# Seven block products for ten input-projection pairs per layer, with the weight sums on GpSimd

## The reference, cut to what matters

```python
h = modulate(rms_norm_2(x, norm1_g), shift1, scale1)
p = h @ w_in                                  # 1024 x 5376
p_ret  = p[..., :RET_COLS]                    # q, k, v, g of the retention mixer
p_rwkv = p[..., RET_COLS:RET_COLS + RWKV_COLS]
p_conv = p[..., RET_COLS + RWKV_COLS:]
q, k, v, g = jnp.split(p_ret, 4, axis=-1)     # rotary on q and k, then retention
gates = jax.nn.sigmoid((h @ w_gate + b_gate).astype(F32))
```

## Time and profile before

| | |
|---|---|
| median of 3 runs | 2393.79 us |
| profiled execution: time, span | 2393.09 us, 2391.3 us |
| TensorE busy | 2263.7 us (95%) |
| weight loads | 1509.1 us (63%) |
| VectorE, ScalarE, GpSimd busy | 675.4, 400.0, 391.6 us |
| granted TensorE clock, mean | 0.992 |

### The profile page before, as it was taken

The page is one execution under the profiler, slowest core; times in us unless marked ns, Lnnn a source line. Parts: engine busy times, 40 slices in busy tenths (PEclk is TensorE's granted clock), DMA queues, the critical chain, the costliest instruction groups (busy, mean ns, idle before and its releaser), DMA issues.

```text
span 2391.3 us, 29443 instructions
## 1 busy us (share of the span) xinstructions
PE 2263.7 (95%) x12878; PEld 1509.1 (63%) x12878; DVE 675.4 (28%) x1225; ACT 400.0 (17%) x787; POOL 391.6 (16%) x347
## 2 busy tenths in 40 slices
PE   9999999999999999999988888899999999888887
PEld 8776676676668888888333333378888863333333
DVE  5532224423216633423100000044443221000001
ACT  3320112620113320211000000033112020000001
POOL 2387631258752000000000000000000000000000
PEclk9999999999999999999999999999999999999999
DMA  7377731358752342349999999953333799999998
GB/s 276 111 310 285 302 137 72 128 213 342 300 202 80 109 141 89 106 160 403 422 428 428 427 428 427 415 197 127 106 108 106 278 406 427 428 428 428 427 428 317
DMA packets 136843, 654.65 MB, mean 274 GB/s; under 512 B 9864, under 2 KB 15112, under 8 KB 108168
## 3 DMA queue, kind: packets, MB, share of 16 engines
q1 hardware_dynamic: 136712, 652.72, 68.4%
HBM read 651.64 MB, written 1.05 MB: 273 GB/s over the span
## 4 chain that ended last, share of the span: by engine, by line
PE 76%; DMA 18%; DVE 2%; ACT 2%; SPq 1%; issue 1%; POOL 0%; DVEq 0%; ACTq 0%; POOLq 0%
PE bank L744 75%; DMA ring<-in_w_exp_up 11%; DMA PRGT<-in_w_exp_up 5%; DMA PRGT<-in_w_exp_down 1%; ACT R L3217 1%; SPq L658 1%; PE bank L1339 0%; DVE sm L2085 0%; POOL PRGT L3315 0%; ACT SQ L3257 0%; DVE PRGT L2416 0%; PE bank L930 0%; DVE PRGT L2079 0%; PE bank L1088 0%; DVE PRGT L2082 0%
## 5 line engine op out<-in xcount | busy, mean ns | idle before, releaser
L744 PE MATMUL bank<-hT,ring 128*128 128x256 f32 x3296 | 733.8, 380 | 0.0
L744 PEld LDWEIGHTS bank<-hT,ring 128*128 128x128 f32 x3296 | 619.8, 190 | 100.2 <-issue 15.3
L744 PE MATMUL bank<-PRGT,R 128*32 128x512 f32 x1120 | 275.9, 609 | 29.9 <-DMA PRGT<-in_w_exp_up 18.5
L744 PE MATMUL bank<-ring,R 128*32 128x512 f32 (+1 forms) x992 | 250.5, 587 | 39.9 <-DMA ring<-in_w_exp_up 25.0
L3393 POOL TENSOR_TENSOR SQ<-xT 128x512 f32<-128x512 f32 x4 | 4.2, 1056 | 1468.5 <-DVE xT L2808 1468.2
L744 PE MATMUL bank<-PRGT,SQ 128*32 128x512 f32 (+2 forms) x864 | 192.5, 530 | 15.6 <-ACT SQ L3257 12.2
L744 PE MATMUL bank<-PRGT,ring 128*128 128x256 f32 (+5 forms) x1136 | 197.0, 373 | 0.4 <-ACT PRGT L3014 0.4
L744 PEld LDWEIGHTS bank<-PRGT,R 128*32 128x32 f32 x1120 | 74.1, 112 | 194.4 <-issue 193.9
L744 PEld LDWEIGHTS bank<-PRGT,ring 128*128 128x128 f32 (+3 forms) x1136 | 163.2, 172 | 31.4 <-issue 3.0
L744 PEld LDWEIGHTS bank<-ring,R 128*32 128x32 f32 (+1 forms) x992 | 69.4, 114 | 168.1 <-issue 167.8
L744 PE MATMUL bank<-ring,SQ 128*32 128x512 f32 (+2 forms) x640 | 167.2, 519 | 8.3 <-ACT SQ L3257 8.3
(11 more groups left out here) (400 smaller groups left out, 2154.3 us busy)
## 6 DMA issues: line engine op xcount, KB each, us to landing
PRGT<-in_w_exp_gate SPq DMA_DIRECT2D x42, 2048.0 KB, 31.9
ring<-in_w_exp_up SPq DMA_DIRECT2D x36, 2048.0 KB, 31.9
ring<-in_mlp_w SPq DMA_DIRECT2D x32, 2048.0 KB, 8.8
PRGT<-in_w_exp_down SPq DMA_DIRECT2D x30, 2048.0 KB, 31.2
PRGT<-in_w_exp_up SPq DMA_DIRECT2D x28, 2048.0 KB, 31.8
PRGT<-in_w_ada SPq DMA_DIRECT2D x32, 1536.0 KB, 11.7
ring<-in_w_exp_down SPq DMA_DIRECT2D x24, 2048.0 KB, 33.3
ring<-in_w_exp_gate SPq DMA_DIRECT2D x22, 2048.0 KB, 32.1
```

The source lines that it names most:

```text
L744: return mm(o, lhsT=lhsT, rhs=rhs, start=first, stop=last, **kw)
```

## The change

Pairs 11 to 20 of each layer (SEVEN) are computed as a 2x2 block product. The contraction (1024 = 2 x 512) and the output (two tiles, and two token halves) are cut in two, and seven products of 512 x 128 x 128 replace eight, at the price of sums: four sums of the activations once a layer (`input_sums`), and four sums of weights a pair (`column_sums`), all on GpSimd and each followed by a semaphore wait of its own. Each product is 4 matmuls of 128 tokens. A pair takes two `acc` banks: four products go to the four 128-column regions of bank n, three go one after the other through the first 128 columns of bank n + 1 (`x`), each copied out by ScalarE (`corners_out`) to a corner buffer in SBUF before the next may overwrite or end it. The first half of a pair now holds four products and the second three. Within the first half the first two products need no sum of the weights, the third waits for the first sum, the fourth for the second.

VectorE puts the pair together (`joined`, three additions, each with one input in PSUM): `joined(10 + j // 2)` at the even steps from 2 on, before the rotary work of that step, then 18 before the turned XX is awaited, and 19 and 20 after the first two levels. GpSimd starts the weight sums behind the first ROWS of the stage; each pair's sums also wait for the weights and for the pair two before it to be nearly done; those of pair 15 also wait for `ret_kq`, the end of the rotary work. ScalarE's order of evictions moves a little. SP's condition for a next load becomes the last product of the pair. Two semaphores are folded into others to make room.

```diff
+SEVEN = tuple(range(11, 21))
...
+        k4 = lambda ap: ap.rearrange("p (k n) -> p k n", k=4)
+        HSUM = [k4(flat(GT[:, 10:12, :])), k4(flat(GT[:, 22:24, :])), k4(hsum3[:, :]), k4(flat(POOL_CD[:, 78:80, :]))]
+        WS = [[k4(flat(YB[:, 6 * b + 2 * r:6 * b + 2 * r + 2, :])) for r in range(3)] for b in range(2)]
+        CORNERS = [small_w[:, 640:1024], flat(stat[:, :, :])[:, 0:384]]
...
+        def h_block(kb, t):
+            return hT[:, 4 * kb:4 * kb + 4, t * P:(t + 1) * P]
+        def w_block(p, kb, h):
+            W = ring[2 + p // 2 % 2][:, 0:(SLOT if p < 20 else 2048)].rearrange("p (k n) -> p k n", k=KT)
+            c = (2 * (p % 2) + h) * P
+            return W[:, 4 * kb:4 * kb + 4, c:c + P]
+        def regions(o):
+            return (o[:, j * P:(j + 1) * P] for j in range(4))
...
+                def seven_products(p, h, o, n):
+                    g = seven_at(l, p)
+                    s1, s2, s4 = WS[g % 2]
+                    t1, t2, t3, t4 = HSUM
+                    z, y1, w, y = regions(o)
+                    m = n + 1
+                    x = acc[m % BANKS][:, 0:P]
+                    def product(dst, lhs, rhs, first=False):
+                        for k in range(4):
+                            ins = mul(dst, lhs[:, k, :], rhs[:, k, :], first and k == 0, False, skip_group_check=True)
+                        return ins
+                    if h == 0:
+                        if m >= BANKS:
+                            pe.wait_ge(dense_read[m % BANKS], m // BANKS)
+                        product(x, w_block(p, 0, 0), h_block(0, 0), True).then_inc(sems["corner_full"], 1)
+                        product(z, w_block(p, 1, 0), h_block(1, 0), True)
+                        pe.wait_ge(sems["sums_ready"], sums_at(l, p) + 1)
+                        product(y, s1, t1)
+                        pe.wait_ge(sems["sums_ready"], sums_at(l, p) + 2)
+                        pe.wait_ge(sems["corner_read"], 2 * g + 1)
+                        product(x, s2, t2).then_inc(sems["corner_full"], 1)
+                    else:
+                        product(w, w_block(p, 1, 1), t4)
+                        pe.wait_ge(sems["sums_ready"], sums_at(l, p) + 3)
+                        product(y1, s4, h_block(1, 1)).then_inc(dense_full[n % BANKS], 1)
+                        pe.wait_ge(sems["sums_ready"], sums_at(l, p) + 4)
+                        pe.wait_ge(sems["corner_read"], 2 * g + 2)
+                        product(x, w_block(p, 0, 1), t3).then_inc(dense_full[m % BANKS], 1)
...
+                def joined(p):
+                    b, full = pair_after(l, p)
+                    m, copied = sum_after(l, p)
+                    o, c = acc[b], CORNERS[seven_at(l, p) % 2]
+                    f0, f1 = (PR[:, in_tiles(p), :][:, h, :] for h in range(2))
+                    dve.wait_ge(dense_full[b], full)
+                    dve.wait_ge(dense_read[m], copied)
+                    v.tensor_tensor(f0, c[:, 0:2 * P], o[:, 0:2 * P], ALU.add)
+                    step(v.tensor_tensor(two(f1), bcast(c[:, 2 * P:3 * P], 2), two(o[:, 2 * P:4 * P]), ALU.add))
+                    v.tensor_tensor(f0[:, P:2 * P], f0[:, P:2 * P], o[:, 3 * P:4 * P], ALU.add).then_inc(dense_read[b], 1)
...
+                    if j >= 2 and j % 2 == 0 and 10 + j // 2 in SEVEN:
+                        joined(10 + j // 2)
...
+                joined(18)
...
+                    if lev < 2:
+                        joined(19 + lev)
...
+                def corners_out(p):
+                    g = seven_at(l, p)
+                    if p in SEVEN[2:]:
+                        b, full = pair_after(l, SEVEN[SEVEN.index(p) - 2])
+                        act.wait_ge(dense_read[b], full)
+                    m, full = sum_after(l, p)
+                    x, c = acc[m][:, 0:P], CORNERS[g % 2]
+                    act.wait_ge(sems["corner_full"], 2 * g + 1)
+                    f(c[:, 0:P], x, ACT.Copy).then_inc(sems["corner_read"], 1)
+                    act.wait_ge(sems["corner_full"], 2 * g + 2)
+                    f(c[:, P:2 * P], x, ACT.Copy).then_inc(sems["corner_read"], 1)
+                    act.wait_ge(dense_full[m], full)
+                    f(c[:, 2 * P:3 * P], x, ACT.Copy).then_inc(dense_read[m], 1)
...
-                for p in range(9, 15):
+                for p in range(9, 16):
                     evict(p)
-                    if p < 12:
-                        swap(p - 8)
+                    if p in (9, 10, 12):
+                        swap({9: 1, 10: 2, 12: 3}[p])
                 n0 = BANK_AT[f"ret_v{l}"]
                 for c in range(TT):
                     copy_out(n0 + c, VT[:, c * 512:(c + 1) * 512])
-                evict(15)
+                evict(16)
                 for p in (14, 15):
                     evicted(p)
                 act.wait_ge(sems["ret_kq"], L.nxt("ret_kq"))
                 f(flat(SIG), flat(PR[:, 12:16, :]), ACT.Sigmoid).then_inc(sems["g_sig"], 1)
-                evict(16)
                 n0 = BANK_AT[f"bonus{l}"]
                 for m in (n0, n0 + 1):
                     act.wait_ge(bank_full[m % BANKS], filled(m))
                 evict(17)
+                evict(18)
                 n0 = BANK_AT[f"turn{l}"]
                 for c in range(TT):
                     copy_out(n0 + c, XTH[c])
-                for p in range(18, 21):
+                for p in range(19, 21):
...
+            def input_sums(l):
+                pool.wait_ge(sems["norm_out"], 46 + KT * l)
+                n = BANK_AT[f"lora{l}"] + 3
+                pool.wait_ge(bank_full[n % BANKS], filled(n))
+                t1, t2, t3, t4 = HSUM
+                b11, b12, b21, b22 = h_block(0, 0), h_block(0, 1), h_block(1, 0), h_block(1, 1)
+                g.tensor_tensor(t1, b12, b11, ALU.subtract).then_inc(sems["sums_ready"], 1)
+                pool.wait_ge(sems["sums_ready"], sums_at(l) + 1)
+                g.tensor_tensor(t2, b22, t1, ALU.subtract).then_inc(sems["sums_ready"], 1)
+                pool.wait_ge(sems["sums_ready"], sums_at(l) + 2)
+                g.tensor_tensor(t3, b22, b12, ALU.subtract).then_inc(sems["sums_ready"], 1)
+                pool.wait_ge(sems["sums_ready"], sums_at(l) + 3)
+                g.tensor_tensor(t4, b21, t2, ALU.subtract).then_inc(sems["sums_ready"], 1)
+                pool.wait_ge(sems["sums_ready"], sums_at(l) + 4)
+            def column_sums(l, p):
+                n, q = seven_at(l, p), p // 2
+                u = SLOT_AT[(f"mid_even{l}", f"mid_odd{l}")[q % 2]][0][1] + q // 2
+                if p % 2 == 0 or p == SEVEN[0]:
+                    pool.wait_ge(slot_full[2 + q % 2], loaded(u))
+                if n >= 2:
+                    b, full = pair_after(*((l, SEVEN[SEVEN.index(p) - 2]) if p in SEVEN[2:] else (l - 1, SEVEN[SEVEN.index(p) - 2])))
+                    pool.wait_ge(dense_full[b], full)
+                s1, s2, s4 = WS[n % 2]
+                a11, a12, a21, a22 = w_block(p, 0, 0), w_block(p, 1, 0), w_block(p, 0, 1), w_block(p, 1, 1)
+                g.tensor_tensor(s1, a21, a22, ALU.add).then_inc(sems["sums_ready"], 1)
+                pool.wait_ge(sems["sums_ready"], sums_at(l, p) + 1)
+                g.tensor_tensor(s2, s1, a11, ALU.subtract).then_inc(sems["sums_ready"], 1)
+                pool.wait_ge(sems["sums_ready"], sums_at(l, p) + 2)
+                g.tensor_tensor(s4, a12, s2, ALU.subtract).then_inc(sems["sums_ready"], 1)
+                pool.wait_ge(sems["sums_ready"], sums_at(l, p) + 3)
+                g.tensor_tensor(a21, a11, a21, ALU.subtract).then_inc(sems["sums_ready"], 1)
+                pool.wait_ge(sems["sums_ready"], sums_at(l, p) + 4)
...
+                input_sums(l)
                 pool.wait_ge(sems["rw_ops"], l + 1)
                 nc.gpsimd.memset(S1[0:64, 256:512], 0.0)
                 nc.gpsimd.memset(S1[64:128, 0:256], 0.0).then_inc(sems["cleared"], 1)
+                pool.wait_ge(sems["cleared"], l + 4)
+                pool.wait_ge(sems["row_ready"], 15 * l + 1)
+                for p in SEVEN:
+                    if p == 15:
+                        pool.wait_ge(sems["ret_kq"], l + 1)
+                    column_sums(l, p)
```

More of the change, by code:

```diff
@@ L236, in nxt, with seven_at, sums_at @@
         return self.seen[name]
+def seven_at(l, p):
+    return len(SEVEN) * l + SEVEN.index(p)
+def sums_at(l, p=None):
+    return 4 * (len(SEVEN) + 1) * l + (0 if p is None else 4 * (SEVEN.index(p) + 1))
+USE_AT, _n = {}, 0
+for _l in range(DEPTH):
+    for _p in range((2, 1)[_l], PAIRS):
+        USE_AT[_l, _p] = _n
+        _n += 1 + (_p in SEVEN)
 def filled(n, i=0):
@@ L256, in pair_after, with sum_after @@
 def pair_after(l, p):
-    n = (PAIRS - 1) * l + p - 2
+    n = USE_AT[l, p]
+    return n % BANKS, n // BANKS + 1
+def sum_after(l, p):
+    n = USE_AT[l, p] + 1
     return n % BANKS, n // BANKS + 1
@@ L294, in build @@
         sm = sb("sm", [P, 512])
+        hsum3 = sb("hsum3", [P, 512])
         CW, W2, W3, ASG = 256, 320, 384, 448
```

(19 more changed lines are left out.)

6 lines of the change are left out of this document (3 added, 3 removed).

## The result

| | kernel before | changed kernel |
|---|---|---|
| median | 2394.0 us (8 runs) | 2401.67 us (8 runs, 2400.49 to 2404.12) |
| profiled execution: time, span | 2393.09, 2391.3 | 2400.49, 2398.7 |
| ratio of the times | | 1.0034, 95% interval 1.0024 to 1.0043 |

It is 0.34% slower. The page of the changed kernel has this line; the line of before is in the earlier trace rows.

A forecast was written before the change was run, and what follows sets the result against it. TensorE, busy 95% of the span, was taken to bound the kernel. 2393.09 - 14.2 (saving) + 23.6 (waits) + 2.0 (clock) = 2404.5 us; the forecast's own range was 2397 to 2413, the overall range 2389 to 2419.

The forecast's parts named there:

- saving of ten pairs: TensorE, pairs 11 to 20: 56 instructions of 0.111 us replace 32 of 0.2167, saving 0.71 a pair, 7.1 a layer.
- after step 5: TensorE's short half (2.87) against VectorE's rotary step (3.47): waits 0.6, plus 1.3 for pair 14's sums hitting rotary work.
- after steps 6 and 7: TensorE waits for VectorE: 0.85 at step 6 (4.62 with the join against 3.76), 0.6 at step 7 (3.47 against 2.87).
- hold at step 8: GpSimd starts pair 15's sums only after the rotary work; TensorE waits 3.7 and another 0.45, together 4.15 us a layer.
- steps 1 to 4: GpSimd's sums for pairs 11 to 14 collide with VectorE's two-input operations: 1.3 us of waits a layer (0 to 4).
- steps 9 to 14: GpSimd's sums are continuous again and collide with VectorE, mostly at step 10: 1.5 us a layer (0 to 6).
- first level: After step 14, sums of pairs 19 and 20 hit VectorE's XX, gating product and four `tensor_scalar`: 1.5 us (0 to 4).
- clock: TensorE's clock falls to half behind the 3.7 us wait for pair 15's sum: 1.0 us a layer (0 to 1.7).
- The rival without collisions (2391.3): GpSimd and VectorE miss each other, clock stays up; 6.2 us of waits remain against 7.1 saved a layer; chance 0.17.
- The rival at 2383: GpSimd's `ret_kq` wait doesn't bite; TensorE keeps its saving except at steps 5 to 7; chance 0.13.
- The one at 2428: Collisions at their upper ends: 22.7 us of waits a layer and 1.7 of clock; chance 0.12 for upper ends.
- the one at 2419: 128-column instructions bound by weight loads add 14.2 us to the forecast; listed under the upper-ends rival, chance 0.12.

The follow-up runs named there:

- short sums: Changed kernel with the weight sums made over only 4 of each 128 columns, outputs not the reference's; 3755.42 us in all, only layer 0's stage compared.
- the filled wait: Changed kernel with pair 15's product that needs no sum done four times instead of once; 2401.10 us, ratio to before 1.0029.
- the join last: Changed kernel with `joined(14)` at step 8 put after `ret_kq` instead of before the rotary operations; 2397.06 us, ratio to before 1.0014.
- without pair 15: Changed kernel with pair 15 back at 32 instructions of 256 columns and GpSimd's `ret_kq` wait ahead of pair 16; 2392.86 us, ratio to before 0.9998.
- pair 13 back in: Changed kernel with only pairs 14 and 15 back at 256 columns, `ret_kq` wait ahead of pair 16; 2386.62 us, ratio to before 0.9970.
- without pairs 13 to 15: Changed kernel with pairs 13, 14 and 15 back at 256 columns, `ret_kq` wait ahead of pair 16; 2384.84 us, ratio to before 0.9962.

## Why the prediction was right, and where its sizes were off

The direction and the mechanism came out as forecast: the order of VectorE's instructions at steps 5 to 8 takes more than the cheaper products give. It forecast 2404.5, 11.4 above the profiled execution of before; that moved by 7.4.

| term, us a layer | predicted | measured, layer 0 / 1 |
|---|---|---|
| saving of ten pairs | 7.1 | 5.2 in the steps, 2.2 / 1.5 in the levels |
| after step 5 | 0.6 + 1.3 | 2.43 / 2.58 |
| after steps 6 and 7 | 0.85 + 0.6 | 0.44 + 0.41 / 0.45 + 0.41 |
| hold at step 8 | 4.15 | 3.45 + 0.18 / 3.46 |
| steps 1 to 4 | 1.3 | 0.0 / 0.4 |
| steps 9 to 14 | 1.5 | 0.3 / 0.3 |
| first level | 1.5 | 0.0 |
| restarts at steps 5 to 8 | not apart | 1.3 / 1.0 |
| clock | 1.0 | 1.7 / 3.0 |

The rows at steps 5 to 8 are idle times; the restarts are what the starts show beside them. The entries for steps 1 to 4 and 9 to 14 are read from starts alone, because a delay shorter than a row's overhang shows no wait: in layer 1 step 2's product starts 0.22 late, at 1671.21, and its row has no bracket. The clock's entries are half of TensorE's busy time in the two windows at 0.51 and 0.50. With 5.2 saved, layer 0's steps come to 63.40 - 5.2 + 6.9 + 1.3 + 0.3 + 1.7 = 68.4 (68.35 measured), layer 1's to 63.41 - 5.2 + 6.9 + 1.0 + 0.7 + 3.0 = 69.8 (69.65).

That the total came within 4 us of the forecast is in part luck, as errors cancel. Over both layers the collisions outside the rotary steps were charged 7.6 us too much, while steps 5 to 8 (1.1), the clock (2.7) and the cheaper pairs (0.8) were all taken too favourably; 0.65 of the last came back in layer 0's levels, with the "issue" wait that went. With the collisions at what they turned out to cost and all else as forecast, the sum would have been 2396.9: still slower, but hardly to be told from no change.

- **Saving.** 0.111 us an instruction was right (8 take 0.89; 864.02 to 864.94 is 0.92). But a half is now several groups with other operands each, and some of them start 0.03 to 0.09 late: two steps and a pair take 6.70 (846.62 to 853.32) against 7.35 before. 0.65 instead of 0.71.
- **Steps 5 to 7 and the hold.** Right as to place and cause. With the restarts, which count as waits in the prediction's reckoning by periods, layer 0 has 0.71 for step 6 (0.85 forecast, with a join of 1.15 that took 1.0), 0.69 for step 7 (0.6) and 4.1 for the hold (4.15). After step 5 it is 2.7 against 1.9: two operations were hit there and not one, in layer 1 too (L2560 and L2561, 1.75 each). The two handovers that it put at 0.1 us took 0.05 (ROWS ready at 869.28, TensorE at 869.33) and 0.13. The hold's chain is shown by three edits: a shorter sum and an earlier `ret_kq` each shorten the wait by about their own length (1.04 and 1.03), and with pair 15 gone it disappears.
- **Collisions.** That GpSimd's sum and VectorE's two-input operation exclude each other was right: short sums take 13.3 us off VectorE in a layer's steps. The step that failed is the one that turned this into waits of TensorE at steps 1 to 4, 9 to 14 and in the first level (4.3 a layer, measured 0.3 and 0.7). It charged two hits of up to 1.27 behind an odd step. VectorE at step 1, in layer 0 and in layer 1, and TensorE in layer 1:

```profile
850.99 0.78 DVE L2553 TENSOR_TENSOR R<-R 128x32 f32<-128x32 f32 x1
851.80 1.31 DVE L2550 TENSOR_SCALAR R<-R,const 128x48 f32<-128x48 f32 x1
...
1668.65 1.16 DVE L2553 TENSOR_TENSOR R<-R 128x32 f32<-128x32 f32 x1
1669.85 1.31 DVE L2550 TENSOR_SCALAR R<-R,const 128x48 f32<-128x48 f32 x1
...
1670.09 1.06 PE L791 MATMUL bank<-hsum,ring 128*128 128x128 f32 x8
1671.21 0.42 PE L791 MATMUL bank<-R,const 128*128 128x48 f32 x2
```

The second hit adds 1.06 in both layers; the first depends on where GpSimd is in its sum, 0.6 in layer 0 and 0.97 in layer 1. TensorE's short half leaves 2.9 us from the start of the step. ROWS was ready after 2.69 in layer 0 (853.11), in time, and after 3.08 in layer 1 (1671.16), where TensorE started 0.22 late. The longest hit on L2553 in layer 0's odd steps is 1.08 (step 5). So 1.05 + 1.08 + 1.06 = 3.2 against 2.9 is a fair estimate of the worst case, 0.3 and not the 0.7 that was charged. In the first level VectorE finished at 922.02 and started on TensorE's first product at 922.05: the gap of 7.97 us that the earlier trace rows shows was used up, but no more. These were near misses, and the prediction's ranges, with their lower ends of 0, allowed for them.
- **The clock** was priced too low. It was also at half for a time behind shorter waits than the hold's: 2.26 us (layer 0 with the filled wait), 2.33 (layer 0 with the join last), 2.41 (short sums), 2.95 (layer 1 without pair 15). The table under "Why this matters for your kernels" in TensorE: Matmul & The Clock Gate, in the Trainium skill, asks for no gaps above about 3 us between bursts. All these waits are below that, while those of 2.43 and 2.58 after step 5 in the changed kernel were followed by no fall. The measurement decides: here a wait under 3 us is not safe, and which of them cost the clock isn't explained by their length alone.

Two readings in the prediction were off and enter no sum: the chain's shares of expert weights in the earlier trace rows add up to 17% and not 18, and there are three joins behind the steps (18, 19, 20), not four.

The rival without collisions (2391.3) is refuted in its cause, since they are there, though their price outside step 5 was small. The rival at 2383 needed the hold not to bite, and it took 3.45 us a layer. The one at 2428 needed sums of 1.5 us or more, and nearly all took 1.27; the one at 2419 needed instructions bound by their weight loads, and 8 of them took 0.89.

## What to carry to other kernels

Trade TensorE's work for another engine's only where that engine has room at that place: price each step by its own cover (the time by which the other engine is done early), not the stage by its mean. VectorE was 55% idle over the steps, and at four of them had 0.3 us to spare. The same scheme on seven of ten pairs made a loss of 0.34% a gain of 0.38%. And where GpSimd makes an operand only after a chain on VectorE has ended, as here, let TensorE need it later: with the hold ahead of pair 16 instead of 15 the wait was gone.

## What the runs showed of the hardware

- A wait of TensorE costs about 0.27 us beyond the idle time in its row: from the starts around the wait after step 5, from two waits with pair 13 back in, and from four without pair 15. A delay shorter than some 0.2 us shows no wait in a row at all.
- A GpSimd sum and a VectorE operation with two SBUF inputs, or a float32 `tensor_scalar`, take turns: 128x512 on VectorE takes 0.69 us alone and up to 1.75 beside a sum of 1.27. The joins, with one PSUM input, took 0.42 beside such sums (854.51, while one ran from 854.49 on) as without them.
- Some builds show a wait of 0.4 to 1.2 us of TensorE in the levels with "issue" as its cause (0.43 before, 0.86 without pairs 13 to 15, none in the changed kernel). Its cause was not looked for. Step 0 of layer 0, too, starts between 846.50 and 848.12 in these builds, for a reason that was not looked for either, and the totals contain it.
- The stage from one layer's levels to the next layer's steps took 707.8 to 708.3 us in every kernel here but the one with short sums, where it wasn't compared, whatever the delay ahead of it.
